# Expert weights in 4 MB transfers and a ring of five buffers, for a hybrid layer with 32 experts

## The reference

```python
def expert_block(args):
    xb, e = args
    hgl = xb @ w1[e] + b1[e]
    glu = jnp.minimum(hgl[:, :D_EXPERT], SWIGLU_LIMIT)
    lin = jnp.clip(hgl[:, D_EXPERT:], -SWIGLU_LIMIT, SWIGLU_LIMIT)
    act = glu * jax.nn.sigmoid(SWIGLU_ALPHA * glu) * (lin + 1.0)
    return act @ w2[e] + b2[e]
```

## Time and profile before

| | |
|---|---|
| median of three runs | 1380.98 us (1380.01 to 1381.06) |
| profiled execution | 1377.24 us |
| its span, first to last instruction | 1375.4 us |
| PE busy | 95% of the span |
| DVE, ACT, POOL busy | 31%, 27%, 3% |
| data moved | 471.33 MB, mean 343 GB/s |
| PE's granted clock | 0.995 of full speed |

### The profile page before, as it was taken

The page is one execution under the profiler, slowest core; times in us unless marked ns, Lnnn a source line. Parts: engine busy times, 40 slices in busy tenths (PEclk is TensorE's granted clock), DMA queues, the critical chain, the costliest instruction groups (busy, mean ns, idle before and its releaser), DMA issues.

```text
span 1375.4 us, 17490 instructions
## 1 busy us (share of the span) xinstructions
PE 1310.5 (95%) x7448; PEld 726.0 (53%) x7448; DVE 427.4 (31%) x810; ACT 364.7 (27%) x558; POOL 34.8 (3%) x57
## 2 busy tenths in 40 slices
PE   6999999999999999999999999999899998899997
PEld 6999999999999433333333333333233333233332
DVE  6765667576553311211111121111121111112111
ACT  5854455654433211111111111111111111111111
POOL 2001200001001000000000000000000000000000
PEclk9999999999999999999999999999999999999999
DMA  7555444359848899999999999999999999999994
GB/s 235 158 152 151 139 143 123 126 183 335 282 148 313 346 402 428 427 428 428 427 427 427 429 426 428 427 428 428 427 427 427 429 428 428 427 427 428 427 429 207
DMA packets 97679, 471.33 MB, mean 343 GB/s; under 512 B 8348, under 2 KB 69928, under 8 KB 71624
## 3 DMA queue, kind: packets, MB, share of 16 engines
q1 hardware_dynamic: 97376, 470.19, 85.2%
q10 hardware_dynamic: 232, 0.07, 0.0%
HBM read 469.19 MB, written 1.05 MB: 342 GB/s over the span
## 4 chain that ended last, share of the span: by engine, by line
PE 67%; DMA 30%; ACT 1%; DVE 1%; issue 0%; DVEq 0%; SPq 0%; ACTq 0%
DMA arena<-in_w_expert_in 30%; PE ps L898 17%; PE ps L925 10%; PE ps L555 7%; PE ps L556 7%; PE ps L557 7%; PE ps L850 3%; PE ps L866 3%; PE ps L546 1%; PE ps L548 1%; PE ps L547 1%; PE ps L858 1%; PE ps L874 1%; PE ps L911 1%; PE ps L907 1%; PE ps L759 1%
## 5 line engine op out<-in xcount | busy, mean ns | idle before, releaser
L898 PE MATMUL ps<-arena 128*64 128x512 f32 x2048 | 455.3, 596 | 43.0 <-DMA arena<-in_w_expert_in 42.6
L898 PEld LDWEIGHTS ps<-arena 128*64 128x64 f32 x2048 | 143.6, 137 | 349.0 <-issue 263.0
L1617 DVE TENSOR_SCALAR arena<-ps 128x512 f32<-128x512 f32 x32 | 22.1, 692 | 683.9 <-PE ps L898 683.9
L925 PE MATMUL ps<-arena 128*64 128x512 f32 x1024 | 226.8, 595 | 0.0
L555 PE MATMUL ps<-A_hi,w_hi 128*128 128x256 f32 x576 | 166.5, 289 | 5.8 <-DVE A_lo L1235 4.5
L556 PE MATMUL ps<-A_lo,w_hi 128*128 128x256 f32 x576 | 163.5, 284 | 0.0
L557 PE MATMUL ps<-A_hi,w_lo 128*128 128x256 f32 x576 | 163.5, 284 | 0.0
L1268 DVE TENSOR_TENSOR w_lo<-w_raw,w_hi 128x1024 fp32r<-128x1024 f32 x120 | 142.7, 1231 | 58.7 <-ACT w_hi L983 58.3
L1199 ACT ACTIVATE arena<-arena 128x512 f32<-128x512 f32 x32 | 20.2, 630 | 460.9 <-DVE arena L1617 460.9
L925 PEld LDWEIGHTS ps<-arena 128*64 128x64 f32 x1024 | 70.7, 137 | 135.7 <-issue 135.7
L983 ACT ACTIVATE w_hi<-w_raw 128x1024 fp32r<-128x1024 f32 x120 | 120.1, 1048 | 24.0 <-DMA w_raw<-in_w_out 7.0
(11 more groups left out here) (305 smaller groups left out, 1342.9 us busy)
## 6 DMA issues: line engine op xcount, KB each, us to landing
arena<-in_w_expert_in SPq DMA_DIRECT2D x120, 2048.0 KB, 45.8
arena<-in_w_expert_out SPq DMA_DIRECT2D x61, 2048.0 KB, 43.6
w_raw<-in_w_in SPq DMA_DIRECT2D x32, 1024.0 KB, 5.5
arena<-in_w_expert_in SPq DMA_DIRECT2D x16, 1024.0 KB, 9.6
w_raw<-in_w_cross_kv SPq DMA_DIRECT2D x8, 1024.0 KB, 7.3
arena<-in_w_expert_out SPq DMA_DIRECT2D x6, 1024.0 KB, 9.2
w_raw<-in_w_ssd_branch SPq DMA_DIRECT2D x4, 1024.0 KB, 5.2
w_raw<-in_w_fox_branch SPq DMA_DIRECT2D x4, 1024.0 KB, 5.2
```

Source lines behind the costliest of these rows:

```text
L898: last = mm(ps[64 * half:64 * (half + 1), b, :], xg_cols[:, 2 * (s % 2) + c, s // 2, :], w[:, at:at + 512], start=False, stop=(s == 3 and ...
L925: last = mm(ps[64 * half:64 * (half + 1), 3, :], at_cols[:, c, s - 4, :], w[:, at:at + 512], start=(s == 4 and c == 0), stop=(s == 5 and c ...
L1617: V_.tensor_scalar(glu, ps[:, 0, :], LIMIT, None, ALU.min).then_inc(glu_ready, 1)
```

## The change

The expert weights are cut into three chunks of 4 MB instead of six of 2 MB. An input chunk has four rows (32 KB) to a partition, so that column 4p+c of the input stands in partition p; this is why the gathered transposes and `prow3` change their strides. The output weights of an expert are one chunk, two runs of 16 KB to a partition. The ring has five slots of four pages and a spare pair (page 23, `X_AT`) that is used once, for the first half of chunk 5. The prefetch still moves 22 MB in pieces of 1 MB, to the same pages in the same order; chunk 5's second half and then all chunks up to 92 follow, each whole (`whole`), and the last expert's three chunks in halves (`half`). SP waits for `e_used`, `h_psum` or `y_psum` of the chunk that had the slot, by its kind; `e_used` now rises once per item, behind the first 32 input matmuls. PE waits once for a whole chunk, and by halves for the first ones and for the last expert.

```diff
-CHUNKS = 6
-SLOTS_W = 11
+CHUNKS = 3
+SLOTS_W = 5
+LAST = CHUNKS * (NE - 1)
...
-        W_AT = (0, 2, 4, 6, 8, 10, 23, 18, 14, 16, 20)
-        prow3 = late[0:4, 1536:1792]
+        W_AT, X_AT = (0, 4, 8, 14, 18), 23
+        prow3 = late[0:2, 1536:2048]
...
-        e_loaded = [sem(f"e_loaded{s}") for s in range(SLOTS_W)]
+        e_loaded = [[sem(f"e_loaded{s}_{h}") for h in range(2)] for s in range(SLOTS_W + 1)]
...
-            if s < 4:
-                return w_ein[0, expert, 256 * s:256 * (s + 1), :].rearrange("(p c) n -> p (c n)", c=2)
-            return w_eout[0, expert, 512 * (s - 4):512 * (s - 3), :].rearrange("(p c) n -> p (c n)", c=4)
-
-        def e_slot(b):
-
-            return page(W_AT[b], 2 * PAGE)
+            if s < 2:
+                return w_ein[0, expert, 512 * s:512 * (s + 1), :].rearrange("(p h c) n -> p h (c n)", h=2, c=2)
+            return w_eout[0, expert].rearrange("(h p c) n -> p h (c n)", h=2, c=4)
+
+        def e_half(n, h):
+
+            at = X_AT if (n, h) == (SLOTS_W, 0) else W_AT[n % SLOTS_W] + 2 * h
+            return page(at, 2 * PAGE)
+
+        def e_sem(n, h):
+            return e_loaded[SLOTS_W if (n, h) == (SLOTS_W, 0) else n % SLOTS_W][h]
+
+        def in_halves(n):
+            return n <= SLOTS_W or n >= LAST
+
+        def e_count(n, h):
+
+            total = 0
+            for m in range(n + 1):
+                if e_sem(m, h) is e_sem(n, h) and (h == 0 or in_halves(m)):
+                    total += 32 if m < SLOTS_W or (m, h) == (SLOTS_W, 0) else 16
+            return total
...
-            def piece(n, h):
-
-                cols = slice(PAGE * h, PAGE * (h + 1))
-                sp_.dma_start(e_slot(n)[:, cols], e_chunk(n // CHUNKS, n % CHUNKS)[:, cols]).then_inc(e_loaded[n], 16)
+            def piece(n, h, k):
+
+                cols = slice(PAGE * k, PAGE * (k + 1))
+                sp_.dma_start(e_half(n, h)[:, cols], e_chunk(n // CHUNKS, n % CHUNKS)[:, h, cols]).then_inc(e_sem(n, h), 16)
+
+            def half(n, h):
+                sp_.dma_start(e_half(n, h), e_chunk(n // CHUNKS, n % CHUNKS)[:, h, :]).then_inc(e_sem(n, h), 16)
+
+            def whole(slot, expert, s):
+
+                to = page(W_AT[slot], 4 * PAGE)
+                if s < 2:
+                    source = w_ein[0, expert, 512 * s:512 * (s + 1), :].rearrange("(p c) n -> p (c n)", c=4)
+                    sp_.dma_start(to, source).then_inc(e_loaded[slot][0], 16)
+                else:
+                    sp_.dma_start(to.rearrange("p (h n) -> p h n", h=2), e_chunk(expert, s)).then_inc(e_loaded[slot][0], 16)
...
-            ahead = [(0, 0), (0, 1), (1, 0), (1, 1), (2, 0), (2, 1), (6, 0), (6, 1)]
+            ahead = [(n, h, k) for n, h in ((0, 0), (0, 1), (1, 0), (5, 0)) for k in range(2)]
             for u in range(unit("out", 3), unit("cv", 1)):
                 load(u)
                 if ahead:
-                    if ahead[0] == (6, 0):
+                    if ahead[0] == (5, 0, 0):
                         sp_.wait_ge(a_lo_ready, SPLIT["u2"] + 4)
                     piece(*ahead.pop(0))
             load(unit("cv", 1))
             sp_.wait_ge(w_done, 2 * unit("cq", 3) + 2)
-            piece(4, 0)
+            piece(2, 0, 0)
             load(unit("cv", 2))
-            piece(4, 1)
+            piece(2, 0, 1)
             for u in range(unit("cv", 3), unit("co", 2)):
                 load(u)
             sp_.wait_ge(xo_psum, X_H)
             load(unit("co", 2))
-            piece(3, 0)
+            piece(1, 1, 0)
             load(unit("co", 3))
-            piece(3, 1)
-            for h in range(2):
-                piece(7, h)
+            piece(1, 1, 1)
+            for k in range(2):
+                piece(4, 0, k)
             sp_.wait_ge(w_lo_ready, 2 * NU)
-            for h in range(2):
-                piece(8, h)
+            for k in range(2):
+                piece(3, 0, k)
             sp_.wait_ge(w_done, 2 * NU)
-            for n in (5, 9):
-                for h in range(2):
-                    piece(n, h)
+            for n in (2, 3):
+                for k in range(2):
+                    piece(n, 1, k)
             sp_.wait_ge(ms_psum, 2)
-            for h in range(2):
-                piece(10, h)
+            for k in range(2):
+                piece(4, 1, k)
             sp_.wait_ge(item_psum, 2)
             sp_.dma_start(b2[0:NE, :], b_eout[0]).then_inc(ld_b2, 16)
             sp_.wait_ge(b1_ready, 2)
             sp_.dma_start(gfin, norm_final_g.partition_broadcast(P)).then_inc(ld_g, 16)
-            for n in range(CHUNKS * NE - SLOTS_W):
-
-                at = n + SLOTS_W
-                sp_.wait_ge(e_used, n + 2)
-                sp_.dma_start(e_slot(at % SLOTS_W), e_chunk(at // CHUNKS, at % CHUNKS)).then_inc(e_loaded[at % SLOTS_W], 16)
+            chunk_used = (e_used, h_psum, y_psum)
+            for n in range(SLOTS_W, CHUNKS * NE):
+                was = n - SLOTS_W
+                sp_.wait_ge(chunk_used[was % CHUNKS], was // CHUNKS + 1)
+                if n == SLOTS_W:
+                    half(n, 1)
+                elif n < LAST:
+                    whole(n % SLOTS_W, n // CHUNKS, n % CHUNKS)
+                else:
+                    half(n, 0)
+                    half(n, 1)
             sp_.wait_ge(meta_ready, 1)
             n_items = sp_.value_load(meta[0:1, NI:NI + 1], min_val=NE, max_val=MAX_ITEMS)
...
                 with sp_.Fori(NE, n_items) as i:
                     e = sp_.value_load(meta[0:1, bass.ds(i, 1)], min_val=0, max_val=NE - 1)
                     for s in range(CHUNKS):
-                        sp_.wait_ge(e_used, CHUNKS * i + (s - 4))
-                        sp_.dma_start(e_slot(s + 5), e_chunk(e, s)).then_inc(e_loaded[s + 5], 16)
...
-            for c in range(2):
-                last = nc.tensor.transpose(ps[:, 3, 136 + 4 * c:140 + 4 * c], prow3[:, c:256:2], ident[0:4, 0:4])
+            for c in range(4):
+                last = nc.tensor.transpose(ps[:, 3, 136 + 2 * c:138 + 2 * c], prow3[:, c:512:4], ident[0:2, 0:2])
...
-                    at = 256 * (m // 2)
-                    last = nc.tensor.transpose(ps[:, 2, m * P:(m + 1) * P], xgs[:, at + m % 2:at + 256:2], idn)
+                    last = nc.tensor.transpose(ps[:, 2, m * P:(m + 1) * P], xgs[:, m:512:4], idn)
...
-            def item(i, slots, loads):
+            def item(i, n, loads):
                 pe.wait_ge(xgt_ready, i + 1)
-                for s in range(4):
-                    pe.wait_ge(e_loaded[slots[s]], loads[s])
-                    w = e_slot(slots[s])
-                    for c in range(2):
+                for s in range(2):
+                    for c in range(4):
+                        if c % 2 == 0 and loads[s][c // 2] is not None:
+                            pe.wait_ge(e_sem(n + s, c // 2), loads[s][c // 2])
+                        w = e_half(n + s, c // 2)
                         for b in range(2):
                             for half in range(2):
-                                at = 2048 * c + b * DE + 512 * half
-                                last = mm(ps[64 * half:64 * (half + 1), b, :], xg_cols[:, 2 * (s % 2) + c, s // 2, :],
-                                          w[:, at:at + 512], start=False, stop=(s == 3 and c == 1), skip_group_check=True)
-                    last.then_inc(h_psum if s == 3 else e_used, 2 if s == 0 else 1)
+                                at = 2048 * (c % 2) + b * DE + 512 * half
+                                last = mm(ps[64 * half:64 * (half + 1), b, :], xg_cols[:, c, s, :],
+                                          w[:, at:at + 512], start=False, stop=(s == 1 and c == 3), skip_group_check=True)
+                    last.then_inc((e_used, h_psum)[s], 1)
                 pe.wait_ge(y_ready, i + 1)
                 pe.wait_ge(sgt_ready, i + 1)
-                scatter().then_inc(e_used, 1)
+                scatter()
                 gather(i + 2)
                 pe.wait_ge(sg_ready, 2 * i + 2)
                 for tb in range(TB):
...
                 pe.wait_ge(at_ready, i + 1)
                 bias(0)
                 pe.wait_ge(sgt_ready, i + 2)
-                for s in range(4, 6):
-                    pe.wait_ge(e_loaded[slots[s]], loads[s])
-                    w = e_slot(slots[s])
+                for h in range(2):
+                    if loads[2][h] is not None:
+                        pe.wait_ge(e_sem(n + 2, h), loads[2][h])
+                    w = e_half(n + 2, h)
                     for c in range(4):
                         for half in range(2):
                             at = D * c + 512 * half
-                            last = mm(ps[64 * half:64 * (half + 1), 3, :], at_cols[:, c, s - 4, :], w[:, at:at + 512],
-                                      start=(s == 4 and c == 0), stop=(s == 5 and c == 3))
-                    last.then_inc(e_used if s < 5 else y_psum, 1)
```

(25 more changed lines are left out.)

## The result

| | before | after |
|---|---|---|
| median of 19 runs each | 1380.64 us (1377.04 to 1381.67) | 1383.14 us (1379.78 to 1385.23) |
| ratio, 95% interval | | 1.0019 [1.0011, 1.0027] |
| profiled execution, its span | 1377.24, 1375.4 us | 1381.81, 1380.1 us |
| span from the first input matmul of expert 0 on | 916.3 us | 920.9 us |

The changed kernel is slower by 2.5 us in the medians, 0.19%, where 3.75 were forecast.

A forecast was written before the change was run, and what follows sets the result against it. The weight stream, late from about 770 us on, was taken to set the end; +6.35 - 3.2 + 0.7 - 0.1 = +3.75 us on a median of 1380.98 us gave 1384.7 us, range 1379.5 to 1389.

The forecast's parts named there:

- The holes: Start of the ring: coarser slots make three holes in the weight stream, putting it 6.35 us later.
- the shift by about two experts: Sign named in the prediction: PE would wait for DMA from about two experts earlier than 770 us.
- The larger transfers: Weight stream, n = 7 to 92: fewer rows and transfer boundaries save 3.2 us, nearly all from input chunks.
- PE late at the end: Experts 30 and 31: after waiting for whole 4 MB chunks, PE reaches the last input half 0.7 us late.
- The small parts: Transposes, a dropped copy ahead of prm_ready, strides, semaphore waits and issues: together -0.1 us, from the copy.
- The fall of the clock in the longer waits: Last stage: PE's 2.7 us waits lower its clock, costing +1.8 us after the last one, 1386.5 us; chance 0.13.
- a fall of the clock in the last stage: Sign against the prediction: it is wrong if the granted clock falls in the last stage.
- rival 2: Input chunk transfers: rows of 32 KB are cut in two and bring nothing, +2.9 us, 1387.6 us; chance 0.14.
- rival 3: Last stage: larger transfers avoid delays from instruction packets sharing the DMA engines, -3.0 us, 1381.7 us; chance 0.12.
- rival 4: Weight stream: rows of 32 KB reach 435 GB/s, saving 12.7 us in place of 3.2, 1375.2 us; chance 0.15.
- rival 5: Weight stream: a fixed price per transfer that the queue does not hide, 87 boundaries save 235 us, 1150 us; chance 0.01.
- rival 6: Output chunk's two rows 2 MB apart, or wider strides between engines, slow the stream by 0.6%, 1390 us; chance 0.03.

## Why the prediction was right

**The holes, +6.35 us.** Right: the issues stood at 466.3, 473.2 and 486.0, three holes, and alone they cost 6.44 us on the stream and 6.5 in the span. The prediction read the chain's 774.7 us as the time from which PE waits; it is the issue of a transfer, and PE waits first at 788.4 us. The term does not hang on it, and the shift by about two experts came (54 us).

**The larger transfers, -3.2 us.** Right in its mechanism, a price for each row and not for each transfer, and mis-sized: 4.1 us. The price of a row had been taken from 1 MB pieces in a stretch of 10 us whose rate is given to 1 GB/s, 0.051 us for 8 rows; it is 0.07. The rounding of that rate alone is worth only 0.006 us, and the rows of 1 KB had given the same 0.05, so why the step to 32 KB saves more for each row is open. By that one term, 0.9 us, the forecast of the end was too late: 3.75 - 0.9 = 2.85, against 2.9 in the profiles (920.9 - 1.7 - 916.3) and 2.5 in the medians. The forecast median of 1384.7 is 1.6 us above the measured one; 0.3 of that comes from its base, 1380.98 from three executions, where 19 gave 1380.64. That the profiled execution, 1381.81 us, came so near its forecast of 1381.0 is luck: the 0.9 us of this term and a fall of the clock worth 1.7 us, which the sum left out, have opposite signs.

**PE late at the end, +0.7 us.** Right: 0.8 to 0.9.

**The small parts, -0.1 us.** The stage of the experts began 0.12 us later, not 0.1 earlier; too little to be read.

**The rivals.** The fall of the clock in the longer waits was real: seven times in one execution, six of them inside PE's slack, the last one worth 1.7 us, as priced. It was set against the forecast as another case with a chance of 0.13, and a fall of the clock in the last stage was named as a sign that the prediction is wrong. That sign came: the granted clock of the last stage was 0.98. The mechanism of the sum stands all the same, and what failed is the either-or: falls come along with the holes and the row price, and cost only in the last wait. Rows of 32 KB cut in two (rival 2) would have given what the run with 16 KB rows gave, 1387.6; they are not cut. The cheaper code loading (rival 3) did not come as far as the trace tells: the stage still has landings that are late (38.93 where 38.41 is usual, at 989.96), but no run took the code loading apart. The stream at 435 GB/s (rival 4) was reached from 497 to 515 us and in single slices, and it was 430 over the last stage; the gain of 0.15 us an expert is a third of what that rival needed. The bare price of a transfer (rival 5) falls with the run in 16 KB rows: half the transfers, no gain. The fit in the Trainium skill's page DMA: Bandwidth & Descriptors (Anatomy of one DMA), about 2.0 us and bytes over 436 GB/s, is given there for single transfers issued by GpSimd; the queued ones of SP here do not follow it. No slower stream (rival 6) was seen.

**What the forecast of the sign rested on.** A gain spread over 86 chunks (4.1 us) and a loss at the start of the ring (6.4 us) worked against each other, and the loss won by 2.2 us on the stream. The sign was right. By the prediction's own border of 0.2% the measured 0.19% is still "same", which it had given 0.21 against 0.63 for slower; with the right row price the sum would have stood at that border.

## What to carry to other kernels

Where a stream of transfers sets the end, find every stretch in which it stands idle, however early and however busy the computing engine is then: each microsecond of it came back at the end here (6.44 us for 6.35 counted). A coarser ring with longer rows saved 9 ns a row over the whole stream here and paid with the idle time until the first coarse slot is free, so use coarse transfers in the long run and fine ones where the ring starts and where the last data are awaited. And before comparing two profiles to 0.1%, cut off what lies ahead of the change: here a clock that falls or not at 195 us moved everything behind it by 3.5 us.

## What the runs showed of the hardware

- A row of a transfer cost 9 ns on its DMA engine beyond its bytes (16 KB rows against 32 KB), and the boundary between queued transfers nothing that could be read (58.73 us for two experts with 4 MB transfers in 16 KB rows and with 2 MB transfers).
- Behind 61 of 92 pieces of idle time of 2.06 to 2.71 us PE's granted clock was at the 1.2 GHz level for a while (0.50 from 763.97 to 766 us in the changed kernel), behind pieces of up to 1.72 us in none; a fall cost 1.7 us of matmuls.
- A row of 32 KB moved as one packet: 128 packets less for each input chunk than in rows of 16 KB.
- Not only idleness did it: 32 matmuls of one column, busy by the page, were followed by some 7 us at 0.52 to 0.56 of the clock in seven traces of eleven, and in neither of the two traces with two parts of 16. By the times, most executions of the kernel before had the fall, and none of the 17 with two parts.
